# RWKV triangular inverse: the level's mask put on by VectorE on the way out of PSUM, the copies of y by ScalarE

## The chip, the cores and the metric

One core of a Trainium2 chip. The kernel is written by hand: each engine (TensorE or PE, VectorE or DVE, ScalarE or ACT, GpSimd or POOL, SyncE or SP) has its own program, and they meet by semaphores. The metric is the time of one execution in microseconds; lower is better.

## What is computed

Two transformer-like blocks of two layers each over 256 tokens of 1024 features, in float32. The second layer of the first block is an RWKV-7 mixer, and its scan is where the change lies:

```python
def frame_step(state, inp):
    r_t, w_t, k_t, v_t, a_t, b_t = inp
    sa = jnp.einsum('bhvk,bhk->bhv', state, a_t)
    state = (state * w_t[:, :, None, :]
             + sa[..., None] * b_t[:, :, None, :]
             + v_t[..., None] * k_t[:, :, None, :])
    y_t = jnp.einsum('bhvk,bhk->bhv', state, r_t)
    return state, y_t
```

It runs over 256 steps for 16 heads of size 64. All else (convolution mixer, MLPs, attention layers) is the same in both kernels.

## The kernel before

**Chunks and slots.** The scan is done in 4 chunks of 64 steps. Inside a chunk the recurrence is a triangular system, whose 64x64 matrix must be inverted for each head and chunk. The 16 heads go through in 4 slots (`SLOTS`) of 4 heads; a slot's work on 128 partitions has two halves, q = 0 and 1, with 4 chunks each. After the 4 slots a fifth round (slot 4) finishes the last slot's chain.

**The inverse.** The Gram matrix comes from TensorE ("gram" step). VectorE masks it: `xt` becomes the inverse of the 2x2 diagonal blocks (the mask of level 0 and the unit matrix, L1992 and L1994), `nb_t` the strictly triangular matrix N beside the products for y (L1995), and a 32x32-block transpose of `xt` gives `inv_x` (L1996). Then the blocks double, level j = 1 to 5. A level has for each half a step "t1", TensorE: `inv_x` times N, with N cut down to the entries that join two blocks of this level (`n_m`), into PSUM; a copy of it to `t1` in SBUF by ScalarE (L1287); a step "dx", TensorE: `t1` times the late columns of `xt`; an addition to `xt` by VectorE (L2005), and a transpose to `inv_x` for the next level (L2008). TensorE's "t1" of level j + 1 waits for that transpose (`inv_ready`), its "dx" for the copy (`t1_out`). The cut N of level 1 is made by VectorE (L1993), that of levels 2 to 5 by GpSimd from `nb_t` (L817, `nm_ready`).

**The chain.** One slot behind, the chain over the 4 chunks runs between these steps: "rhs", "u", "sy". ScalarE takes the results of "rhs" and "u" out of PSUM (L1293, L1301) and scales the old state (L1298); VectorE makes the new state (L2020, L2022) and copies y out of PSUM, three copies for each chunk (`keep_y`, L1980 and L1982, 48 in all), at the step "u" of the next chunk. "sy" of the next chunk waits for them (`y_out`).

**What sets the order.** `wkv_steps(slot)` is one list of steps which TensorE, ScalarE and VectorE all walk through, each in order and each waiting by semaphore. Other work is hung on places in it. In slot 0 that is, on TensorE, the last value projections (L2252 to L2254), and on VectorE `mixer_inputs(3)`, which prepares slot 3 (L1882 and L1883 after level 1, L1885 and L1887 after level 2, L1889 after level 3, all 128x512), and two halves of weight splits (`w_lo`, L1507, 128x1024, after level 4 and at the end). In slots 1 and 2 there is one such half, between the two "t1" steps of level 3. Slots 2 and 3 have the group norm of finished heads as well (L1965, L1968, L1971, L1974). Slot 4 has the first rows of the output projection, for which VectorE makes `z_lo` (L1956).

**GpSimd** has an order of its own: in each slot the masks of levels 2 to 5, and between them the inputs of the next slot (`build_bk`: L761, L763; `build_ar`: L774 to L776; then it adds to `built`), and after them `gate_products` of this slot (L783, L784, L787), all 128x512 in SBUF.

## Time and profile before

| | us |
|---|---|
| median of 3 runs | 1352.33 |
| lowest, highest run | 1350.98, 1352.74 |
| span of the profiled execution (first to last instruction) | 1350.7 |
| its stretch with slots 0 to 4 of the scan (about 427 to 549 us) | 122 |

The profiled execution lasts 1350.7 us from its first to its last instruction; the median of the runs is 1.6 us more, for what lies around the span. In it slot 0 begins with the gram step at 426.93 us, and slots 1 to 3 begin at 455.02, 478.26 and 503.07 us; the chain of slot 3 begins at 527.7 us. TensorE has the full clock in all of them. A row of the timeline gives the start in microseconds, the duration, the engine and the line; neighbouring instructions of one line are merged into a row with xN; what stands in brackets is the idle time of the engine ahead of the row and what ended it. PE's own rows are modelled and overlap, so that a wait of some tenths of a microsecond can hide in the tail of the row ahead. A few PE records are missing.

### The profile page before, as it was taken

To read this page: it belongs to the slowest core of one execution; us is meant where nothing else is said; L and a number is where in the kernel's file an instruction comes from. 1 tells how busy PE (TensorE), PEld (TensorE's weight loads), DVE (VectorE), ACT (ScalarE), POOL (GpSimd) and SP (SyncE) were. 2 spreads that over 40 slices of the span, in tenths; PEclk is the share of its full clock that TensorE was granted. 3 is DMA by queue.
4 is the path that set the end of the run, shared out by engine and by line. 5 is a ranking of instruction groups with operands and counts; after the bars stand their busy time and mean duration, and the time that the engine had idled before them with its cause. 6 is when DMAs were issued, how large, how long until landed. Compare 5 with 4: busy or idle time off the path is not lost. (4 is left out here: it accounts for less than half of the span.)

```text
span 1350.7 us, 24951 instructions
## 1 busy us (share of the span) xinstructions
PE 1303.9 (97%) x10507; PEld 1130.7 (84%) x10507; DVE 948.4 (70%) x1433; ACT 701.1 (52%) x1211; POOL 128.3 (9%) x133
## 2 busy tenths in 40 slices
PE   4999999999999999999999999999999999999997
PEld 2998888997899887788888887888888998888886
DVE  1887788976768776685556888666657677756655
ACT  2534544434467455564444648654445566644443
POOL 0000000010200864100000142000000021000000
PEclk9999999999999999999999999999999999999999
DMA  9997899995341012356665532465565544565561
GB/s 363 373 366 236 302 350 381 356 344 161 110 156 64 4 35 97 98 178 196 188 192 177 176 121 74 150 203 192 187 196 160 170 143 126 172 188 192 183 197 51
DMA packets 177559, 256.90 MB, mean 190 GB/s; under 512 B 10472, under 2 KB 122536, under 8 KB 177448
## 3 DMA queue, kind: packets, MB, share of 16 engines
q1 hardware_dynamic: 177448, 255.31, 57.0%
q8 instruction: 83, 1.36, 0.4%
q14 instruction: 28, 0.23, 0.0%
HBM read 254.25 MB, written 1.05 MB: 189 GB/s over the span
## 5 line engine op out<-in xcount | busy, mean ns | idle before, releaser
L1507 DVE TENSOR_TENSOR w_lo<-stage,w_hi 128x1024 fp32r<-128x1024 f32 (+1 forms) x372 | 447.3, 1238 | 160.4 <-ACT w_hi L882 160.0
L882 ACT ACTIVATE w_hi<-stage 128x1024 fp32r<-128x1024 f32 (+1 forms) x378 | 379.9, 1049 | 211.7 <-PE acc L2311 191.9
L2309 PE MATMUL acc<-w_hi,z_hi 128*128 128x512 f32 x640 | 252.7, 395 | 1.6 <-DVE z_lo L1956 1.6
L2311 PE MATMUL acc<-w_hi,z_lo 128*128 128x512 f32 x640 | 249.4, 390 | 0.0
L2310 PE MATMUL acc<-w_lo,z_hi 128*128 128x512 f32 x640 | 249.2, 389 | 0.0
L2252 PE MATMUL un<-h_both,w_hi 128*128 128x256 f32 x736 | 214.9, 292 | 1.8 <-POOL w_lo L853 1.1
L2253 PE MATMUL un<-h_both,w_hi 128*128 128x256 f32 x736 | 208.8, 284 | 0.0
L2254 PE MATMUL un<-h_both,w_lo 128*128 128x256 f32 x736 | 208.8, 284 | 0.0
L2252 PEld LDWEIGHTS un<-h_both,w_hi 128*128 128x128 f32 x736 | 141.6, 192 | 9.5 <-issue 5.4
L2309 PEld LDWEIGHTS acc<-w_hi,z_hi 128*128 128x128 f32 x640 | 120.1, 188 | 27.8 <-issue 3.9
L2253 PEld LDWEIGHTS un<-h_both,w_hi 128*128 128x128 f32 x736 | 141.7, 193 | 1.2 <-issue 0.7
L2254 PEld LDWEIGHTS un<-h_both,w_lo 128*128 128x128 f32 x736 | 141.7, 193 | 0.0
L2311 PEld LDWEIGHTS acc<-w_hi,z_lo 128*128 128x128 f32 x640 | 120.1, 188 | 25.4
L2310 PEld LDWEIGHTS acc<-w_lo,z_hi 128*128 128x128 f32 x640 | 120.2, 188 | 23.4
L2290 PE MATMUL un<-h_both,w_hi 128*128 128x512 f32 x384 | 121.2, 397 | 0.4 <-DVE w_lo L1507 0.4
L2290 PE MATMUL side<-h_both,w_hi 128*128 128x512 f32 x384 | 120.8, 396 | 0.4
L2293 PEld LDWEIGHTS side<-h_both,w_lo 128*128 128x128 f32 x384 | 72.1, 188 | 17.0
L2293 PEld LDWEIGHTS un<-h_both,w_lo 128*128 128x128 f32 x384 | 72.1, 188 | 16.9
L2293 PE MATMUL un<-h_both,w_lo 128*128 128x256 f32 x384 | 75.5, 278 | 0.0
L2293 PE MATMUL side<-h_both,w_lo 128*128 128x256 f32 x384 | 75.5, 278 | 0.0
L1789 DVE SCALAR_TENSOR_TENSOR ada_sum<-ada_buf,small,ada_sum 128x1024 f32<-128x1024 f32 x49 | 62.8, 1282 | 1.0
L2290 PEld LDWEIGHTS un<-h_both,w_hi 128*128 128x128 f32 x384 | 59.1, 189 | 1.7 <-DVE w_lo L1507 0.6
(393 smaller groups left out, 1885.1 us busy)
## 6 DMA issues: line engine op xcount, KB each, us to landing
stage<-in_mlp_w SPq DMA_DIRECT2D x64, 1024.0 KB
ada_buf<-in_ada_w SPq DMA_DIRECT2D x48, 1024.0 KB, 11.1
stage<-in_w_up SPq DMA_DIRECT2D x32, 1024.0 KB
stage<-in_w_down SPq DMA_DIRECT2D x32, 1024.0 KB
...
```

Of the source, the lines that this page charges most:

```text
L882: A_(w_hi[u % 2][:, half, 0:n], stage[u % NSTAGE][:, half, 0:n], ACT.Copy).then_inc(hi_made, 1)
L1507: V.tensor_tensor(w_lo[u % 2][:, half, 0:n], stage[u % NSTAGE][:, half, 0:n], w_hi[u % 2][:, half, 0:n].bitcast(F32), ALU.subtract).then_i ...
L1789: V.scalar_tensor_tensor(out=to[:], in0=rows, scalar=by, in1=to[:], op0=ALU.mult, op1=ALU.add).then_inc(ada_weighed, 1)
L2252: MM(out, hi_l, hi_r, start=start, stop=False, skip_group_check=True)
L2253: MM(out, hi_l, lo_r, start=False, stop=False, skip_group_check=True)
L2254: return MM(out, lo_l, hi_r, start=False, stop=stop, skip_group_check=True)
L2290: MM(pair[:, m, :, :], wh[:, kt, c], h_both[:, kt, :, :], start=(kt == 0), stop=False, skip_group_check=True)
L2293: ins = MM(pair[:, m, 0, :], wl[:, kt, c], h_hi[:, kt, :], start=False, stop=(kt == KT - 1), skip_group_check=True)
L2309: MM(y, z_hi[:, kt, q], wh[:, i, :], start=(first and kt == 0), stop=False, skip_group_check=True)
L2310: MM(y, z_hi[:, kt, q], wl[:, i, :], start=False, stop=False, skip_group_check=True)
L2311: ins = MM(y, z_lo[:, kt, q], wh[:, i, :], start=False, stop=(last and kt == KT - 1), skip_group_check=True)
```

## The change

Three things move. The matrix N is no longer cut for each level: TensorE's "t1" takes `nb_t` itself, and the mask of the level (`level_of`, turned) is multiplied onto the product when it leaves PSUM. This multiplication is VectorE's; ScalarE's 40 copies of `t1` go, and so do GpSimd's 32 masks, VectorE's 8 and the buffers `n_m`. The 48 copies of y go from VectorE to ScalarE, at the same steps. GpSimd's other work now stands at the head of its slot. TensorE's instructions stay as they are but for one operand and one wait.

```diff
-    levels = [(s >> (j + 1) == q >> (j + 1)) & ((q >> j) & 1 == 1) & ((s >> j) & 1 == 0) for j in range(6)]
-    put("level_t", np.stack(levels, 1))
+    paired = lambda early, late, j: (early >> (j + 1) == late >> (j + 1)) & ((late >> j) & 1 == 1) & ((early >> j) & 1 == 0)
+    put("level_first", paired(s, q, 0))
+    put("level_of", np.stack([paired(q, s, j) for j in range(1, 6)], 1))
...
@@ -780,10 +780,13 @@
+                pool.wait_ge(built, s + 1)
+                pool.wait_ge(chain_input, 3)
                 link(G.tensor_tensor(rw_c[:, t, :], rw_r[:, t, :], rw_k[:, t, :], ALU.mult))
                 G.tensor_tensor(rw_c[:, t, :], rw_c[:, t, :], spread(VEC_RK), ALU.mult).then_inc(rk_ready, 1)
                 if s == 0:
                     pool.wait_ge(lora2_out, 20)
+                    pool.wait_ge(built, 1)
...
@@ -808,24 +811,15 @@
             for s in range(SLOTS):
-                for j in WKV_LEVELS[1:]:
-                    for q in range(2):
-                        if j == 2:
-                            pool.wait_ge(inv_ready, 12 * s + q + 1)
-                        else:
-                            pool.wait_ge(t1_done, 10 * s + 2 * (j - 3) + q + 1)
-                        G.tensor_tensor(n_m[(j - 1) % 2][:, q, :, :], nb_t[s % 2][:, q, :, 0:CHUNK],
-                                        level_t[:, j, :].unsqueeze(1).to_broadcast([P, CHUNKS, CHUNK]), ALU.mult).then_inc(nm_ready, 1)
-                    if j == (2 if s else 4) and s + 1 < SLOTS:
-                        build_bk(s + 1)
-                    if j == (3 if s else 5) and s + 1 < SLOTS:
-                        build_ar(s + 1)
-                    if j == 4 and s >= 2:
-                        group_weigh(s - 2)
+                if s + 1 < SLOTS:
+                    build_bk(s + 1)
+                    build_ar(s + 1)
+                if s >= 2:
+                    group_weigh(s - 2)
+                gate_products(s)
                 if s >= 2:
                     group_gate(s - 2)
                     group_add(s - 2)
-                gate_products(s)
...
@@ -1273,6 +1267,15 @@
+            def keep_y(s, c):
+
+                act.wait_ge(y_done, CHUNKS * s + c + 1)
+                cols = slice(CHUNK * c, CHUNK * (c + 1))
+                A_(y_wkv[:, 2 * s, cols], two_pairs(misc, P)[:, 0, :], ACT.Copy)
+                for rows, to in zip(HEAD, HEAD[::-1]):
+                    ins = A_(y_wkv[to, 2 * s + 1, cols], two_pairs(misc, P)[rows, 1, :], ACT.Copy)
+                ins.then_inc(y_out, 1)
...
@@ -1283,8 +1286,6 @@
                     elif step == "t1":
-                        act.wait_ge(t1_done, 10 * s + 2 * (j - 1) + q + 1)
-                        A_(t1[:, q, :, :], half_bank(acc[q], 0), ACT.Copy).then_inc(t1_out, 1)
...
@@ -1299,6 +1300,10 @@
                         A_(wkv_u[:], two_pairs(stat_ps, P), ACT.Copy).then_inc(u_out, 1)
+                        if j:
+                            keep_y(s, j - 1)
+                    elif step == "sy" and j == CHUNKS - 1:
+                        keep_y(s, j)
...
@@ -1989,15 +1985,18 @@
-                        V.tensor_tensor(xt, raw_n[:, :, 0:CHUNK], bc4(level_t[:, 0, :], CHUNKS), ALU.mult)
-                        link(V.tensor_tensor(n_m[0][:, q, :, :], raw_n[:, :, 0:CHUNK], bc4(level_t[:, 1, :], CHUNKS), ALU.mult))
-                        V.tensor_tensor(xt, xt, bc4(eye, CHUNKS), ALU.add)
+                        V.tensor_tensor(xt, raw_n[:, :, 0:CHUNK], bc4(level_first, CHUNKS), ALU.mult)
                         link(V.tensor_tensor(nb_t[s % 2][:, q, :, :], raw_n, bc4(c_("masks"), CHUNKS), ALU.mult))
+                        link(V.tensor_tensor(xt, xt, bc4(eye, CHUNKS), ALU.add))
...
+                    elif step == "t1":
+
+                        dve.wait_ge(t1_done, 10 * s + 2 * (j - 1) + q + 1)
+                        V.tensor_tensor(t1[:, q, :, :], half_bank(acc[q], 0), bc4(level_of[:, j - 1, :], CHUNKS), ALU.mult).then_inc(t1_out, 1)
...
@@ -2022,10 +2021,6 @@
-                        else:
-                            keep_y(s, c)
-                    elif step == "u" and j:
-                        keep_y(s, j - 1)
...
@@ -2689,10 +2684,8 @@
                         pe.wait_ge(inv_ready, 12 * s + 2 * (j - 1) + q + 1)
-                        if j > 1:
-                            pe.wait_ge(nm_ready, 8 * s + 2 * (j - 2) + q + 1)
                         for c in range(CHUNKS):
-                            ins = by_head(half_bank(acc[q], 0)[:, c, :], n_m[(j - 1) % 2][:, q, c, :], xn[:, c, :])
+                            ins = by_head(half_bank(acc[q], 0)[:, c, :], nb_t[i][:, q, c, 0:CHUNK], xn[:, c, :])
```

The order on VectorE in slot 0, from the end of `mixer_inputs(2)` to the next piece, before. `acc0` to `acc3` are PSUM banks (0 and 1 hold "t1", 2 and 3 "dx"), `tmp` and `rw0` to `rw5` the mixer's tiles in SBUF:

```order
L1889 SCALAR_TENSOR_TENSOR rw4_115<-rw4_115,rw5_116 128x512
L2005 TENSOR_TENSOR inv_t2_189<-acc2,inv_t2_189 128x64x2 [waits dx_done,chain_input]
L2008 STREAM_TRANSPOSE inv_x_142<-inv_t2_189 128x256 [waits dve_chain]
L2005 TENSOR_TENSOR inv_t2_189<-acc3,inv_t2_189 128x64x2 [waits dx_done]
L2008 STREAM_TRANSPOSE inv_x_142<-inv_t2_189 128x256 [waits dve_chain]
L1882 TENSOR_TENSOR tmp_61<-tmp_61,ss_inv_126 128x512 [waits ss_root,ss_ready]
L1883 SCALAR_TENSOR_TENSOR tmp_61<-tmp_61 128x512 [waits dve_chain]
L2005 TENSOR_TENSOR inv_t2_189<-acc2,inv_t2_189 128x32x4 [waits dx_done,dve_chain]
L2008 STREAM_TRANSPOSE inv_x_142<-inv_t2_189 128x256 [waits dve_chain]
```

and in the changed kernel:

```order
L1894 SCALAR_TENSOR_TENSOR rw4_115<-rw4_115,rw5_116 128x512
L1999 TENSOR_TENSOR t1_150<-acc0,const1_64 128x256 [waits t1_done,chain_input]
L1999 TENSOR_TENSOR t1_150<-acc1,const1_64 128x256 [waits t1_done]
L2004 TENSOR_TENSOR inv_t2_187<-acc2,inv_t2_187 128x64x2 [waits dx_done]
L2007 STREAM_TRANSPOSE inv_x_142<-inv_t2_187 128x256 [waits dve_chain]
L2004 TENSOR_TENSOR inv_t2_187<-acc3,inv_t2_187 128x64x2 [waits dx_done]
L2007 STREAM_TRANSPOSE inv_x_142<-inv_t2_187 128x256 [waits dve_chain]
L1887 TENSOR_TENSOR tmp_61<-tmp_61,ss_inv_126 128x512 [waits ss_root,ss_ready]
L1888 SCALAR_TENSOR_TENSOR tmp_61<-tmp_61 128x512 [waits dve_chain]
L1999 TENSOR_TENSOR t1_150<-acc0,const1_64 128x256 [waits t1_done,dve_chain]
L1999 TENSOR_TENSOR t1_150<-acc1,const1_64 128x256 [waits t1_done]
L2004 TENSOR_TENSOR inv_t2_187<-acc2,inv_t2_187 128x32x4 [waits dx_done]
```

The two multiplications L1999 stand ahead of each level's additions, and behind `mixer_inputs` (L1887 and L1888 here are L1882 and L1883 before).

The order on GpSimd in slot 0, before:

```order
L817 TENSOR_TENSOR n_m1_145<-nb_t0_133,const1_64 128x256 [waits const_mid_in,inv_ready,un_free,rw_ready]
L817 TENSOR_TENSOR n_m1_145<-nb_t0_133,const1_64 128x256 [waits inv_ready]
L817 TENSOR_TENSOR n_m0_144<-nb_t0_133,const1_64 128x256 [waits t1_done] x2
L817 TENSOR_TENSOR n_m1_145<-nb_t0_133,const1_64 128x256 [waits t1_done] x2
L761 TENSOR_TENSOR b_fm_138<-rw4_115,w_inv_141 128x512 [waits tok_done,exp_ready,rw_ready]
L763 TENSOR_TENSOR k_fm_139<-rw1_112,w_inv_141 128x512
L817 TENSOR_TENSOR n_m0_144<-nb_t0_133,const1_64 128x256 [waits t1_done] x2
L774 COPY ar1_143<-rw5_116 128x8
```

and in the changed kernel, where the inputs of slot 1 and then the gate products come first:

```order
L761 TENSOR_TENSOR b_fm_138<-rw4_115,w_inv_141 128x512 [waits rw_ready,exp_ready,const_mid_in,tok_done,un_free]
L763 TENSOR_TENSOR k_fm_139<-rw1_112,w_inv_141 128x512
L774 COPY ar1_143<-rw5_116 128x8
L775 TENSOR_TENSOR ar1_143<-rw5_116,w_cum_140 128x8x63
L776 TENSOR_TENSOR ar1_143<-rw0_111,w_cum_140 128x8x64
L777 ISA [waits pool_chain]
L785 TENSOR_TENSOR rw3_114<-rw0_111,rw1_112 128x512 [waits chain_input,built]
L786 TENSOR_TENSOR rw3_114<-rw3_114,vecT_66 128x512 [waits pool_chain]
L790 TENSOR_TENSOR rw1_112<-sq_62,vecT_66 128x512 [waits built,lora2_out]
```

The eight masks that this piece had between and ahead of them are gone, and nothing in it waits for a level of the inverse.

ScalarE in slot 1, level 3, from the chain's "rhs" of chunk 2 to that of chunk 3, before:

```order
L1293 ACTIVATE wkv_rhs_149<-side 128x128 [waits rhs_done]
L882 ACTIVATE w_hi1_54<-stage1_50 128x1024 [waits unit_done,unit_landed1]
L1287 ACTIVATE t1_152<-acc0 128x256 [waits t1_done]
L1298 ACTIVATE state_kept_148<-state1_147,w_end_151 128x64 [waits state_ready]
L1298 ACTIVATE state_kept_148<-state1_147,w_end_151 128x64
L1301 ACTIVATE wkv_u_150<-side 128x128 [waits u_done]
L1287 ACTIVATE t1_152<-acc1 128x256 [waits t1_done]
L1287 ACTIVATE t1_152<-acc0 128x256 [waits t1_done]
L1293 ACTIVATE wkv_rhs_149<-side 128x128 [waits rhs_done]
```

and in the changed kernel:

```order
L1294 ACTIVATE wkv_rhs_147<-side 128x128 [waits rhs_done]
L876 ACTIVATE w_hi1_54<-stage1_50 128x1024 [waits unit_done,unit_landed1]
L1299 ACTIVATE state_kept_146<-state1_145,w_end_149 128x64 [waits state_ready]
L1299 ACTIVATE state_kept_146<-state1_145,w_end_149 128x64
L1302 ACTIVATE wkv_u_148<-side 128x128 [waits u_done]
L1274 ACTIVATE tmp_61<-side 128x64 [waits y_done]
L1276 ACTIVATE tmp_61<-side 64x64 x2
L1294 ACTIVATE wkv_rhs_147<-side 128x128 [waits rhs_done]
```

Three copies of y now stand behind `wkv_u`, and the copies of `t1` are gone.

## Rows read from the trace of the kernel before

**Rows 1.** The page, busy time of the engines, with the number of their instructions.

```profile
PE 1303.9 (97%) x10507; PEld 1130.7 (84%) x10507; DVE 948.4 (70%) x1433; ACT 701.1 (52%) x1211; POOL 128.3 (9%) x133
```

**Rows 2.** Windows, slots 0 to 3: length; PE, PEld, DVE, ACT, POOL busy; clock; DMA.

```profile
426.93:455.02 28.09, 27.37 (x574) 25.29 (x574) 23.42 (x43) 17.56 (x36) 14.09 (x14) 1.00 0.01 3
455.02:478.26 23.24, 21.05 (x712) 19.96 (x709) 18.32 (x51) 12.21 (x33) 18.38 (x19) 1.00 0.03 5
478.26:503.07 24.81, 22.76 (x722) 21.31 (x719) 18.67 (x52) 14.43 (x38) 14.18 (x15) 1.00 0.12 46
503.07:527.14 24.07, 22.73 (x720) 21.22 (x716) 18.91 (x53) 12.75 (x35) 12.92 (x14) 1.00 0.05 7
```

**Rows 3.** Groups by line and shape, 426 to 545 us: busy, mean ns | idle before.

```profile
L817 POOL TENSOR_TENSOR n_m<-nb_t,const 128x256 f32<-128x256 f32 x32 | 25.7, 820 | 102.6 <-DVE inv_x L1996 89.5 <-PE acc L2642 12.9
...
L1287 ACT ACTIVATE t<-acc 128x256 f32<-128x256 f32 x40 | 15.3, 383 | 30.3 <-PE acc L2642 30.0
...
L1982 DVE COPY tmp<-side 64x64 f32<-64x64 f32 x30 | 6.7, 222 | 0.4
...
L1301 ACT ACTIVATE wkv_u<-side 128x128 f32<-128x128 f32 x15 | 4.1, 275 | 5.7 <-PE side L2642 5.6
...
L1993 DVE TENSOR_TENSOR n_m<-acc,const 128x256 f32<-128x256 f32 x8 | 3.3, 409 | 0.0
...
L1980 DVE COPY tmp<-side 128x64 f32<-128x64 f32 x15 | 3.1, 208 | 2.2 <-PE side L2642 2.1
```

**Rows 4.** Timeline of slot 0, ScalarE: start, microseconds, line, operation.

```profile
437.83 0.62 ACT L1141 ACTIVATE w_inv<-rw 128x512 f32<-128x512 f32 x1
...
440.17 0.38 ACT L1287 ACTIVATE t<-acc 128x256 f32<-128x256 f32 x1 [1.72 <-PE acc L2642]
```

**Rows 5.** Timeline of slot 0, VectorE.

```profile
438.89 0.68 DVE L1889 SCALAR_TENSOR_TENSOR rw<-rw,rw 128x512 f32<-128x512 f32 x1
...
442.85 0.65 DVE L1882 TENSOR_TENSOR tmp<-tmp,ss_inv 128x512 f32<-128x512 f32 x1
...
443.53 0.69 DVE L1883 SCALAR_TENSOR_TENSOR tmp<-tmp 128x512 f32<-128x512 f32 x1
...
444.89 0.29 DVE L2005 TENSOR_TENSOR inv_t<-acc,inv_t 128x128 f32<-128x128 f32 x1 [0.67 <-PE acc L2642]
...
446.24 1.04 DVE L1885 SCALAR_TENSOR_TENSOR rw<-rw,tmp 128x512 f32<-128x512 f32 x1
...
447.32 1.64 DVE L1887 SCALAR_TENSOR_TENSOR rw<-ka_mix,rw 128x512 f32<-128x512 f32 x1
...
450.22 0.70 DVE L1889 SCALAR_TENSOR_TENSOR rw<-rw,rw 128x512 f32<-128x512 f32 x1
```

**Rows 6.** Timeline of slot 0, GpSimd and TensorE.

```profile
446.69 1.72 POOL L763 TENSOR_TENSOR k_fm<-rw,w_inv 128x512 f32<-128x512 f32 x1
...
444.12 1.12 PE L2642 MATMUL acc<-inv_t,t 64*64 64x32 f32 x32
```

**Rows 7.** Timeline of slot 1, VectorE and, last, TensorE.

```profile
457.61 0.41 DVE L1992 TENSOR_TENSOR inv_t<-acc,const 128x256 f32<-128x256 f32 x1
...
462.05 0.43 DVE L2020 TENSOR_SCALAR state<-side,w_end 128x64 f32<-128x64 f32 x2
...
462.40 1.28 DVE L2000 TENSOR_TENSOR nk_t<-acc,const 128x512 f32<-128x512 f32 x2
...
463.40 0.61 PE L2642 MATMUL acc<-inv_t,t 64*64 64x32 f32 x16
```

**Rows 8.** Timeline of slots 1 to 4, VectorE.

```profile
470.01 1.25 DVE L1507 TENSOR_TENSOR w_lo<-stage,w_hi 128x1024 fp32r<-128x1024 f32 x1 [0.33 <-ACT w_hi L882]
...
497.85 0.68 DVE L1968 SCALAR_TENSOR_TENSOR rw<-un,rw 128x512 f32<-128x512 f32 x1
...
505.04 1.13 DVE L1994 TENSOR_TENSOR inv_t<-inv_t,const 128x256 f32<-128x256 f32 x1
...
530.84 3.20 DVE L1956 TENSOR_TENSOR z_lo<-rw,z_hi 128x512 fp32r<-128x512 f32 x2
```

More of the change, by code:

```diff
@@ L49 @@
 CONST_PARTS = ((("ident", P), ("mean", P), ("ones", P), ("rot", P)),
-               (("head_ones", P), ("head_mean", P), ("level_t", 6 * CHUNK), ("masks", 2 * CHUNK), ("eye", CHUNK), ("resets", SEQ),
+               (("head_ones", P), ("head_mean", P), ("level_first", CHUNK), ("level_of", 5 * CHUNK), ("masks", 2 * CHUNK), ("eye", CHUNK), ("resets", SEQ),
                 ("eye_centered", CHUNK)),
@@ L169, in build @@
         ident, mean_w, ones_w, head_ones, head_mean, rot_w = (c_(n) for n in ("ident", "mean", "ones", "head_ones", "head_mean", "rot"))
-        level_t = c_("level_t").rearrange("p (j q) -> p j q", j=6)
+        level_first, level_of = c_("level_first"), c_("level_of").rearrange("p (j q) -> p j q", j=5)
         eye, eye_centered = c_("eye"), c_("eye_centered")
@@ L259, in build @@
         ar.append(scratch_new("ar1", DOUBLE))
-        n_m = [scratch_new(f"n_m{i}", PACKED) for i in range(2)]
         state = [scratch_new(f"state{i}", [P, 2, HD]) for i in range(2)]
@@ L712, in build @@
             sem(n) for n in ("g_done", "v_done", "gk_done", "tok_done", "tok_out", "inv_ready", "lak_ready", "chain_input"))
-        nm_ready, t1_done, t1_out, dx_done = (sem(n) for n in ("nm_ready", "t1_done", "t1_out", "dx_done"))
+        t1_done, t1_out, dx_done = (sem(n) for n in ("t1_done", "t1_out", "dx_done"))
         rhs_done, rhs_out, u_done, u_out, y_done, y_out, s_done, state_ready = (
@@ L1974, in group_step @@
                     V.scalar_tensor_tensor(out=rw_k[:, t, :], in0=rw_k[:, t, :], scalar=-0.5, in1=s, op0=ALU.mult, op1=ALU.mult).then_inc(scaled, 1)
-            def keep_y(s, c):
-                dve.wait_ge(y_done, CHUNKS * s + c + 1)
-                cols = slice(CHUNK * c, CHUNK * (c + 1))
-                V.tensor_copy(y_wkv[:, 2 * s, cols], two_pairs(misc, P)[:, 0, :])
-                for rows, to in zip(HEAD, HEAD[::-1]):
-                    ins = V.tensor_copy(y_wkv[to, 2 * s + 1, cols], two_pairs(misc, P)[rows, 1, :])
-                ins.then_inc(y_out, 1)
             for slot in range(SLOTS + 1):
```

## The prediction

> **What bounds the kernel now.** I read the page first, then the windows of the scan's slots, then the timeline slot by slot. On the page TensorE is busy for 97% of the span [rows 1], so time is won or lost only where TensorE waits, or is kept waiting longer. The change touches nothing outside the scan. In its slots TensorE's rows cover 27.4 of 28.1, 21.1 of 23.2, 22.8 of 24.8 and 22.7 of 24.1 us [rows 2], about 6 us open in all, and VectorE's 23.4, 18.3, 18.7 and 18.9 us: it is the second engine, well ahead of ScalarE (17.6, 12.2, 14.4, 12.8 us). The reader is to see that the change takes work from engines with room (GpSimd 14 to 18 us a slot, ScalarE) and puts 40 instructions on the one with least room, inside the loop that releases TensorE. After the scan TensorE's work goes on without a gap that could take up a delay; I let a shift go through to the end.
>
> **The prices.** A multiplication of the mask is a VectorE tensor_tensor with one operand in PSUM, 128x256. L1993 is exactly that: 0.41 us [rows 3]. ScalarE's copy takes 0.38 [rows 3], so the exchange by itself costs TensorE 0.03 us. VectorE gets 40 x 0.41 = 16.4 us, and loses 8 x 0.41 = 3.3 and 16 copies of y at 0.21 + 2 x 0.22 = 0.65, 10.4 us: net +2.7 us. But slot 0 has no copies of y, and gets 10 x 0.41 - 2 x 0.41 = +3.3 us on 23.4 of 28.1. ScalarE loses 15.3 us, and gets the copies of y; the trace has no ScalarE copy of 64 columns. Its nearest row is `wkv_u`, 128 columns, 0.28 us [rows 3]: at most 3 x 0.28 = 0.83 a chunk, at least VectorE's 0.65; I take 0.7. [...] GpSimd loses 25.7 us of masks [rows 3]. The waits name no GpSimd instruction that TensorE waited for, so this gives nothing directly; what it does to VectorE comes below.
>
> **Slot 0, VectorE in the loop.** Before, ScalarE copied `t1` at 440.17 [rows 4], and while VectorE was in `mixer_inputs` ScalarE did level 2's copies beside it: "dx" could go at 444.12 [rows 6], though VectorE was in L1882 and L1883 from 442.85 to 444.22 [rows 5]. Now these multiplications stand behind them in VectorE's queue. A level becomes a serial piece: first multiplication 0.41, then "dx" to the first addition 444.12 to 444.89 = 0.77 [rows 5, 6], then two additions and two transposes, 444.89 to 446.24 = 1.35 [rows 5]: 2.53 us, the second multiplication and the second "dx" lying inside. From the first product at 440.15: four levels, 10.1; the last without transposes, 0.41 + 0.77 and 0.65 for two additions, 1.85; the mixer pieces 1.37, 1.37 and 0.69; two weight splits at 1.25 [rows 8]. Sum 17.9, so gram of slot 1 would begin on VectorE at 458.05 and not at 457.61 [rows 7]: +0.45.
>
> That is without GpSimd. L1887 took 1.64 us where its like take 0.69; GpSimd's L763 ran until 446.69 + 1.72 = 448.41, and L1887 ended 0.55 behind that [rows 5, 6]. L763 itself had waited for L1885. So such a pair, both reading two operands from SBUF, goes by turns. The change starts GpSimd's stream for slot 1 when `w_inv` is there, 438.45 [rows 4], where L763, the second piece of it, started at 446.69 before. It has no more masks to break it: seven pieces of 1.05 to 1.2 us (L763's 1.72 less its wait) and a short copy, until about 449. By turns I get: L1889, due 438.89 [rows 5], ends at 440.7 (the first multiplication 0.55 late); level 1 to 443.25; L1882 by 443.95, L1883 waits for L776 until 445.2 and ends at 445.75; level 2 to 448.3; L1885 waits for the last gate product until 449.1, L1887 ends at 450.3; level 3 452.8; L1889 453.5; level 4 456.05; split 457.3; level 5 459.15; split 460.4. Against 457.61 that is +2.8. The ends from the rows: VectorE loses nothing where it comes first (L1889 at 450.22, 0.70 us [rows 5]), +0.45; it loses L1887's 0.95 at each of the five meetings, +0.45 + 4.75 = +5.2. I take the walk, since its turns are those of L1885 and L1887.
>
> [...]
>
> **Slots 1 to 3.** The gram step loses L1993 twice, 0.8 us. But "dx" of level 1 must now wait behind the new state, both `nk_t` and a multiplication. Before: gram begins 457.61, its last transpose makes way at 462.05, `nk_t` begins 462.40 for 1.28, "dx" goes at 463.40, 5.8 after the start [rows 7]. Now: 4.44 - 0.8 + 0.35 + 1.25 + 0.4 = 5.65. The 0.8 us are nearly all given back: -0.15. The weight split between the two "t1" steps of level 3 (470.01, 1.25 us [rows 8]) now stands ahead of a multiplication too. Before, the same copy stood on ScalarE behind its own share of that split, so it was late too; I take 0.3 of the 1.25 as new. The copies of y on ScalarE stay hidden, as two steps lie between "u" and "sy". Slot 1 is +0.15 in all, and slot 2 +0.2, where the group's work leaves TensorE less to wait for. L1968 (0.68 us [rows 8]) stands behind the second multiplication of level 4 in slots 2 and 3, which waits for its product; the addition behind it comes some 0.4 late: +0.3 and +0.4. Slot 3 begins with GpSimd on the group's sum, its weights and the gate products, five pieces or some 6 us in a row; L1994 met one of them before (1.13 for 0.43 [rows 8]), and now both halves do, 0.6 + 0.7 for 0.7: +0.6; the copies of y that VectorE drops at the end of the slot give back 0.4. Slots 1 to 3: 0.15 + 0.5 + 0.6 = +1.25.
>
> **Slot 4.** `z_lo` took 3.20 us for two because GpSimd's gate products ran [rows 8]; these are done earlier now, so 1.4. TensorE had other work for most of it: -0.35.
>
> **Sum.** +2.8 + 1.25 - 0.35 = +3.7 us on a span of 1350.7; the median of the runs is 1.6 above the span, so 1352.3 + 3.7 = 1356.0 us. Its own range is 1354.6 to 1358.
>
> **The rivals.**
> *The locks miss.* If GpSimd's pieces fall between VectorE's, slot 0 costs 0.45 and slot 3 nothing: 0.45 + 0.8 - 0.35 = +0.9, 1353.2 us. For it: L1889 at 450.22 was not stretched [rows 5], though GpSimd ran. Against: GpSimd has no gap for 10 us and VectorE comes to it five times.
> *The cleared gram step is kept (faster).* If "dx" of level 1 in slots 1 to 3 is not held by VectorE but by the transpose alone, the 0.8 us stay in each: -2.4; with slot 4's -0.35, L1994's 0.7 of slot 3 [rows 8] gone as well, and slot 0 even: -3.45, 1348.9 us. It decides at whether VectorE comes to the multiplication before TensorE has its level 1 product and "rhs" behind it, that is within 1.3 us of the last transpose (462.05 to 463.40); I count 0.35 + 1.25 + 0.4 = 2.0 [rows 7].
> *ScalarE holds the chain (slower still).* `y_out` comes 0.7 us after `u_out` now, and "sy" needs it at its start and not at its middle. If that is exposed at half of the 12 places in slots 1 to 4 that have a chain step behind, 6 x 0.5 = +3 on top: 1359 us. Against: two steps of TensorE lie between.
>
> **The numbers.** Main case 0.52, locks miss 0.24, faster 0.12, slower still 0.12. About 0.2%, 2.7 us, is what a measurement of this kernel can tell from no change. The main case lies above 1355.0 for the most part (0.45 of 0.52), so slower is 0.45 + 0.12 + 0.02 = 0.59; same 0.07 + 0.22 = 0.29; faster 0.12. The range 1351.8 to 1358.8 leaves out the faster case and half of the last.
>
> **What would show it.** Slot 1's gram step on TensorE begins near 458.5 in the span's time (455.02 before), if slot 0 is right; VectorE's L1883 (now L1888) of slot 0 lasts about 1.8 us and shows the lock, 0.7 would show that it misses. In slot 1 the distance from gram's first VectorE row to the first "dx" is 5.65 us; 5.0 would be the faster rival. `z_lo` in slot 4 takes 1.4 us. Waits of TensorE for `tmp` of ScalarE at "sy" would show the last rival. I am wrong at the root if TensorE's waits in slot 0 stay under 1 us, or if a multiplication takes much else than 0.41 us.

## The result and the profile after

The changed kernel is slower: 1358.07 us median of four runs (1357.15 to 1362.24) beside 1352.26 for the kernel before on the same chip, a ratio of 1.0052, 95% interval 1.0036 to 1.0067, so +5.8 us where +3.7 was forecast. The direction was right, the size too small; the time lies inside the range by 0.7 us, and only since the range reached toward the slowest rival.

The profiled execution of after is the slowest of the four (span 1360.5 us, against 1350.7 before; its mean granted clock is 0.993, that of the other three 0.995 or 0.996), so it shows more loss than the median has. The table compares the stage slot by slot, from VectorE's first gram row of a slot to that of the next; the last column runs from slot 3's first gram row to the row of VectorE that begins the chain's last new state in slot 4.

| us | slot 0 | slot 1 | slot 2 | slot 3 and chain |
|---|---|---|---|---|
| before | 29.42 | 21.91 | 24.73 | 37.55 |
| after | 34.87 | 22.21 | 25.39 | 38.36 |
| difference | +5.45 | +0.30 | +0.66 | +0.81 |

That is +7.2 us, three quarters of it in slot 0. Another 1.0 us lies ahead of the stage and some 1.6 behind it, where both kernels run the same instructions; behind the stage the profiles of all kernels here spread by 3 us, so the 1.6 says nothing on the change.

The windows of after: slot 0, slot 1, and four pieces of slot 0 (length; busy PE, PEld, DVE, ACT, POOL; granted clock; DMA).

```profile
428.00:462.50 34.50, 31.20 (x578) 29.27 (x582) 27.29 (x51) 15.11 (x26) 9.08 (x8) 0.85 0.01 3
462.50:485.10 22.60, 20.58 (x714) 19.74 (x712) 18.43 (x47) 10.36 (x33) 8.39 (x8) 1.00 0.02 4
...
444.00:448.00 4.00, 1.29 (x42) 1.15 (x38) 3.86 (x4) 0.00 (x0) 3.77 (x3) 0.98 0.00 0
448.00:452.00 4.00, 4.00 (x54) 3.71 (x54) 2.74 (x6) 0.00 (x0) 1.03 (x2) 0.50 0.01 2
452.00:456.00 4.00, 4.00 (x56) 3.81 (x52) 2.90 (x7) 0.00 (x0) 0.00 (x0) 0.50 0.02 4
456.00:458.00 2.00, 2.00 (x37) 1.91 (x38) 0.42 (x1) 0.00 (x0) 0.00 (x0) 0.50 0.00 0
```

Before, slot 0 had TensorE busy for 27.37 of 28.09 us at clock 1.00 [rows 2]. Now two things are there that were not. From 444 to 448 TensorE is busy for 1.29 of 4 us. Behind it the granted clock is 0.50 for 10 us (0.85 over 34.5 us says the same: 34.5 x 0.15 / 0.5 = 10.4).

What TensorE waited for stands in the timeline of after, GpSimd, VectorE and TensorE around 444 us:

```profile
443.65 1.27 POOL L776 TENSOR_TENSOR ar<-rw,w_cum 128x512 f32<-128x512 f32 x1
445.07 1.52 POOL L785 TENSOR_TENSOR rw<-rw,rw 128x512 f32<-128x512 f32 x1 [0.15 <-POOLq L777]
...
443.88 1.59 DVE L1887 TENSOR_TENSOR tmp<-tmp,ss_inv 128x512 f32<-128x512 f32 x1
445.50 1.63 DVE L1888 SCALAR_TENSOR_TENSOR tmp<-tmp 128x512 f32<-128x512 f32 x1
447.17 0.76 DVE L1999 TENSOR_TENSOR t<-acc,const 128x256 f32<-128x256 f32 x2
...
443.79 1.15 PE L2637 MATMUL acc<-inv_x,nb_t 64*64 64x64 f32 x32
447.65 1.05 PE L2637 MATMUL acc<-inv_t,t 64*64 64x32 f32 x18 [2.71 <-DVE t L1999]
```

L1887 and L1888, the mixer's pieces, took 0.65 and 0.69 us before [rows 5]. Each now ends 0.55 us behind the end of the GpSimd instruction that runs at its start (444.92 and 446.59). The multiplication L1999 stands behind them in VectorE's queue, and "dx" starts 3.86 us after "t1" did, with 2.71 us of idle time.

In slot 1 the gram step is 0.8 us lighter, and the first "dx" comes no earlier than before: 469.91 - 464.08 = 5.83 us (5.79 before [rows 7]). VectorE's first gram row, its `nk_t` and its multiplication, and TensorE's "dx":

```profile
464.08 0.42 DVE L1988 TENSOR_TENSOR inv_t<-acc,const 128x256 f32<-128x256 f32 x1
...
468.15 1.28 DVE L1995 TENSOR_TENSOR nk_t<-acc,const 128x512 f32<-128x512 f32 x2
469.35 0.75 DVE L1999 TENSOR_TENSOR t<-acc,const 128x256 f32<-128x256 f32 x2
...
469.91 0.50 PE L2637 MATMUL acc<-inv_t,t 64*64 64x32 f32 x11 [0.59 <-DVE t L1999]
```

The copies of y on ScalarE (`tmp` is where y is kept), and "sy" that waits for them, later in slot 1:

```profile
475.40 1.05 ACT L876 ACTIVATE w_hi<-stage 128x1024 fp32r<-128x1024 f32 x1
476.35 0.57 ACT L1299 ACTIVATE state_kept<-state,w_end 128x64 f32<-128x64 f32 x2
476.83 0.26 ACT L1302 ACTIVATE wkv_u<-side 128x128 f32<-128x128 f32 x1
476.99 0.22 ACT L1274 ACTIVATE tmp<-side 128x64 f32<-128x64 f32 x1
477.21 0.45 ACT L1276 ACTIVATE tmp<-side 64x64 f32<-64x64 f32 x2
...
477.72 0.45 PE L2637 MATMUL side<-v_tok,bk_tok 64*64 64x64 f32 x8 [0.65 <-ACT tmp L1276]
```

The groups of after by line, in the stage (busy, mean ns | idle before):

```profile
L1999 DVE TENSOR_TENSOR t<-acc,const 128x256 f32<-128x256 f32 x40 | 16.3, 417 | 9.1 <-PE acc L2637 8.8
L1276 ACT ACTIVATE tmp<-side 64x64 f32<-64x64 f32 x32 | 7.0, 219 | 0.4
...
L2637 PEld LDWEIGHTS side<-v_tok,bk_tok 64*64 64x64 f32 x96 | 3.8, 134 | 2.8 <-ACT tmp L1276 2.7
L1274 ACT ACTIVATE tmp<-side 128x64 f32<-128x64 f32 x16 | 3.5, 219 | 2.7 <-PE side L2637 2.7
```

Before, the same weight loads of "sy" stood idle for 0.8 us, of which 0.4 for VectorE's copies of y:

```profile
L2642 PEld LDWEIGHTS side<-v_tok,bk_tok 64*64 64x64 f32 x96 | 3.9, 134 | 0.8 <-DVE tmp L1982 0.4 <-issue 0.3
```

### The profile page after: what moved, and what is told of

It reads as the page before. It is cut to its first block and busy times, and to the rows that moved or that the text cites. A ratio compares the mean times of both kernels' runs of the same rounds, so it can differ in the third digit from the quotient of the medians.

```text
span 1360.5 us, 24884 instructions
## 1 busy us (share of the span) xinstructions
PE 1308.1 (96%) x10507; PEld 1135.0 (83%) x10507; DVE 949.8 (70%) x1417; ACT 697.9 (51%) x1219; POOL 102.9 (8%) x101
## 3 DMA queue, kind: packets, MB, share of 16 engines
HBM read 254.25 MB, written 1.05 MB: 188 GB/s over the span
```

## Experiments

Theory A: slot 0 is long because GpSimd's stream stretches VectorE's pieces, the multiplication comes late, TensorE waits, and the clock falls behind that wait. Rivals: VectorE's queue alone does it (B); the clock has another cause (C). More rivals, with letters of their own, stand with the run that tests them. For slots 1 to 4: ScalarE's copies of y hold the chain (E), or VectorE's sum of work is the price (F). The totals are medians, with the kernel before run beside them on the same chip; the slots are read from one profiled execution of each kernel.

| kernel | us, before beside it | ratio, 95% | slot 0 | slot 1 | slot 2 | slot 3 and chain |
|---|---|---|---|---|---|---|
| pool_late | 1355.00, 1351.48 | 1.0025 (1.0016 to 1.0034) | 30.04 | 22.21 | 25.37 | 38.37 |
| warm | 1364.17, 1351.48 | 1.0086 (1.0072 to 1.0100) | 35.85 | 22.21 | 27.40 | 38.37 |
| warm3 | 1358.51, 1351.99 | 1.0047 (1.0034 to 1.0059) | 31.57 | 22.21 | 25.61 | 38.39 |
| b_idle | 1356.47, 1350.95 | 1.0038 (1.0026 to 1.0050) | 32.49 | 21.85 | 24.62 | 37.54 |
| moved | 1355.56, 1351.99 | 1.0026 (1.0015 to 1.0037) | 29.97 | 22.25 | 25.50 | 38.35 |
| moved_late | 1354.13, 1351.99 | 1.0019 (1.0010 to 1.0027) | 28.72 | 22.25 | 25.77 | 38.36 |
| moved_split | 1354.33, 1351.99 | 1.0019 (1.0010 to 1.0027) | 28.71 | 22.94 | 24.93 | 38.35 |
| y_back | 1359.09, 1351.48 | 1.0059 (1.0047 to 1.0072) | 33.53 | 22.87 | 25.94 | 39.04 |
| b_y_act | 1354.40, 1351.48 | 1.0024 (1.0015 to 1.0033) | 29.43 | 22.63 | 25.41 | 38.33 |
| y_first | 1356.19, 1351.31 | 1.0037 (1.0023 to 1.0051) | 32.37 | 22.04 | 25.12 | 37.83 |
| b_y_first | 1353.30, 1351.31 | 1.0012 (1.0003 to 1.0021) | 29.43 | 23.58 | 24.82 | 37.78 |
| b_all | 1352.37, 1351.31 | 1.0010 (1.0001 to 1.0018) | 29.20 | 23.59 | 25.28 | 37.79 |
| inter | 1357.93, 1351.87 | 1.0048 (1.0034 to 1.0062) | 32.34 | 21.62 | 25.38 | 37.76 |
| all_three | 1352.38, 1351.31 | 1.0008 (0.9999 to 1.0016) | 28.72 | 22.07 | 24.86 | 37.80 |
| four | 1352.04, 1351.87 | 1.0005 (0.9996 to 1.0013) | 29.19 | 21.79 | 24.74 | 37.23 |
| four_s | 1351.81, 1350.95 | 1.0004 (0.9996 to 1.0013) | 28.70 | 21.80 | 25.00 | 37.21 |
| five | 1351.00, 1350.95 | 0.9997 (0.9988 to 1.0006) | 28.38 | 22.49 | 24.87 | 37.24 |

### GpSimd's stream late (pool_late)

```diff
             for s in range(SLOTS):
+                if s == 0:
+                    pool.wait_ge(t1_done, 6)
                 if s + 1 < SLOTS:
                     build_bk(s + 1)
                     build_ar(s + 1)
```

> The changed kernel with one edit: in slot 0 GpSimd starts its stream (inputs of slot 1, then gate products) only when the two products of level 3 are there, as late as the masks of the kernel before let it. Theory A (the lock and what it does to the clock): L1887 and L1888 of slot 0 last 0.69 us each and not 1.59 and 1.63, TensorE's wait ahead of the second level's "dx" falls from 2.7 us to about 1, and its granted clock stays at 1.00 through slot 0; the later pieces of GpSimd meet L1894 and the weight split and cost about 1 us. Slot 0 lasts 29 to 30 us and not 34.5, the total is 1353 to 1354.5 us. Rival B (VectorE's queue is enough): the pieces standing ahead of the multiplications starve TensorE with or without GpSimd, the clock falls all the same, slot 0 stays over 33 us and the total at 1357 or more.

Slot 0 is 30.04 us long, at the upper end of what Theory A gave, and the total 0.5 us above its range. The clock is 1.00 throughout. VectorE's pieces at level 2 and GpSimd's first one, in its timeline (the line numbers are two higher here):

```profile
442.90 0.65 DVE L1889 TENSOR_TENSOR tmp<-tmp,ss_inv 128x512 f32<-128x512 f32 x1
443.59 0.69 DVE L1890 SCALAR_TENSOR_TENSOR tmp<-tmp 128x512 f32<-128x512 f32 x1
...
448.21 1.26 POOL L761 TENSOR_TENSOR b_fm<-rw,w_inv 128x512 f32<-128x512 f32 x1 [95.32 <-PE acc L2639]
```

With no GpSimd beside them the same two instructions take 1.34 and not 3.22 us. Rival B falls: 4.8 us of the profiled slot 0 come and go with the order of GpSimd alone.

### The wait filled, and the clock with it (warm, warm3)

```diff
+                if n == 9:
+                    pe.wait_ge(tok_out, 4)
+                    unread(un[0], 3)
                 if n in (7, 11, 15, 19):
                     value_rows(3, misc, ...)
```

(`warm` has 8 for 3; `n == 9` is the second "t1" of level 2.)

> The changed kernel with eight matmuls of 128x512 more on TensorE between level 2's "t1" and "dx" of slot 0, into a free PSUM bank that nothing reads: they fill the wait and alter no data. VectorE and GpSimd do the same work as in the changed kernel. Theory A (the wait itself costs what the walk said, and the clock the rest): the clock stays at 1.00 in slot 0, L1887 and L1888 still take 1.6 us each, slot 0 lasts 28.1 + 2.8 = 31 us, the total is 1354 to 1355 us. Rival C (the fall of the clock has nothing to do with this wait, or the later waits bring it as well): half clock is still seen in slot 0 and the total stays at 1357 to 1358.5. Rival D (the matmuls hold the chain up): at half a microsecond each they could last longer than the wait, then "dx" starts later than 447.8 and the total is above 1358.

Rival D came true: sixteen rows of 0.45 us lasted 7.13 us, "dx" started only at 453.04, and slot 0 took 35.85 us, at clock 1.00. (Its slot 2 is long, 27.40 us, for a fall of its own: the clock is 0.61 from 492 to 496 us.) So three were taken:

> As the run with eight added matmuls, but three of them in the same place: eight lasted 7.13 us (sixteen rows of 0.45) and outlasted the wait, three make 2.7 us, which is TensorE's wait there in the changed kernel (444.94 to 447.65). VectorE and GpSimd do what they do in the changed kernel, and "dx" starts when it did. Theory A (the waits cost what the walk said, the fall of the clock costs the rest): the granted clock stays 1.00 in slot 0, slot 0 (from VectorE's first gram row to that of slot 1) lasts 31.5 us and not 34.87, and the total is 3.3 us under that of the changed kernel, some 1354 us. Rival C (this wait doesn't decide the clock): half clock is still seen before slot 1, slot 0 stays over 34 us, the total within 1 us of the changed kernel's.

The timeline of warm3, VectorE and TensorE, and its windows (as above):

```profile
444.87 1.59 DVE L1887 TENSOR_TENSOR tmp<-tmp,ss_inv 128x512 f32<-128x512 f32 x1
446.50 1.64 DVE L1888 SCALAR_TENSOR_TENSOR tmp<-tmp 128x512 f32<-128x512 f32 x1
...
445.87 2.84 PE L2351 MATMUL un<-const 128*128 128x512 f32 x6
448.65 1.06 PE L2640 MATMUL acc<-inv_t,t 64*64 64x32 f32 x30
...
429.00:460.20 31.20, 29.69 (x584) 26.16 (x588) 26.82 (x51) 15.11 (x26) 9.08 (x8) 1.00 0.01 3
...
450.00:454.00 4.00, 3.29 (x74) 2.98 (x73) 3.47 (x10) 0.00 (x0) 0.04 (x1) 1.00 0.02 6
```

VectorE and GpSimd do exactly what they do in after, "dx" comes 3.78 us behind L1887's start (3.77 in after), only TensorE is not idle meanwhile. The clock stays at 1.00, and slot 0 takes 31.57 us, not 34.87. This splits slot 0's +5.45 in the profiled executions: the waits cost 31.57 - 29.42 = 2.15 us, the half clock 3.3 us. Rival C falls.

The total did not come down as Theory A had it: 1358.5 us, where 1354 was expected. So the 3.3 us rest on one profile of each kernel, and no median shows them. The profiled execution begins the stage 2.0 us late, with a clock of 0.67 between 340 and 344 us, long before anything that differs. The profiles of warm, y_back and five show a fall at the same place (0.66, 0.59 and 0.69), those of the other kernels, before and after among them, do not, so it does not come from the added matmuls. The fastest run (1356.17 us, mean clock 0.998) is what the slot lengths give (1352 + 4.2). The others had 0.996 or 0.997. Why the clock falls there in some executions and not in others is open.

### The same wait in the kernel before (b_idle)

```diff
                     elif step == "t1":
                         act.wait_ge(t1_done, 10 * s + 2 * (j - 1) + q + 1)
+                        for _ in range(6 if (s, j, q) == (0, 2, 0) else 0):
+                            link(A_(t1[:, q, :, :], half_bank(acc[q], 0), ACT.Copy))
                         A_(t1[:, q, :, :], half_bank(acc[q], 0), ACT.Copy).then_inc(t1_out, 1)
```

> The kernel before with ScalarE's first copy of t1 at level 2 of slot 0 done seven times over instead of once (same data each time), some 3 us more between that "t1" and its "dx". Masks, GpSimd's order and VectorE's pieces are those of the kernel before, so nothing is stretched but this one wait of TensorE. Theory A (a wait of this size in slot 0 brings the granted clock down to half behind it): TensorE waits 2.5 to 3.5 us there, half clock of 3 to 10 us follows, slot 0 is longer by the wait and 1 to 3 us more; total +4 to +6. Rival C (the clock needs the changed kernel's other waits too): clock 1.00, slot 0 longer by 2.5 to 3 us and no more.

Its timeline, ScalarE's six copies and TensorE's "dx", and two windows:

```profile
443.83 2.46 ACT L1288 ACTIVATE t<-acc 128x256 f32<-128x256 f32 x6 [1.87 <-PE acc L2644]
...
446.76 1.12 PE L2644 MATMUL acc<-inv_t,t 64*64 64x32 f32 x32 [2.51 <-ACT t L1289]
...
444.00:448.00 4.00, 1.49 (x43) 1.31 (x38) 0.81 (x3) 2.79 (x8) 4.00 (x4) 0.97 0.00 0
448.00:452.00 4.00, 3.95 (x60) 3.62 (x62) 2.36 (x6) 0.97 (x3) 1.39 (x3) 0.60 0.02 4
```

A wait of 2.51 us, with nothing else changed, and the clock is at half behind it. Theory A holds for the cause. The median rose by 5.5 us, about twice the wait. Slot 0 grew by 3.07 us, the wait and 0.6 more, under the 1 to 3 that Theory A gave: this execution had half clock for 3.2 us only. All six runs took 1353.8 to 1358.8 us, and their mean clocks order them: 0.997 for the two fastest, 0.995 for the next three, 0.994 for the slowest.

### Pieces out of slot 0 (moved, moved_late, moved_split)

```diff
-                if slot == 0 and n in (7, 11, 15):
-                    mixer_inputs(3, (n // 4 - 1,))
+                if slot == 0 and n in (7, 11):
+                    mixer_piece(3, (0, 3)[(7, 11).index(n)])
+                if slot == 1 and n in (13, 25, 31):
+                    mixer_piece(3, (1, 2, 4)[(13, 25, 31).index(n)])
```

(`mixer_piece(k, i)` is instruction i of the five of `mixer_inputs`. The first and fourth read `ss_inv` and `ka_mix`, whose memory slot 1 writes over.)

> The changed kernel with mixer_inputs(3) taken apart: in slot 0 only L1887 (after level 1) and L1892 (after level 2) stay, L1888, L1890 and L1894 go to slot 1, after level 1's second addition, between level 4's "t1" steps and between level 5's, where VectorE waits for 0.4 to 0.7 us. GpSimd's order stays as in the changed kernel. Theory A: VectorE has one piece less to meet GpSimd with at level 2, L1887 still takes 1.6 us but L1888 is gone, TensorE's wait there is 1.1 us and not 2.7, the clock stays at 1.00: slot 0 about 29.5 to 30.5, slot 1 some 0.5 us longer, total 1353.5 to 1354.5. Rival B (one stretched piece is enough): the clock falls all the same, over 1356.

> Both edits together: the pieces in slot 1 as in that run, and GpSimd's stream of slot 0 held until level 3's products. Theory A: no piece is stretched at level 2, slot 0 has 2.05 us less of VectorE's work on its loop than with the late stream alone (30.04 us there) and lasts 28.5 to 29, slot 1 0.5 longer than 22.2; total 0.5 to 1.5 us under that with the late stream alone, 1353.5 to 1354.5. Rival G (slot 1 has no room: each piece there delays a multiplication for its whole 0.69 us): what slot 0 gives, slot 1 takes, total as with the late stream alone.

> As moved_late, and slot 1's half of a weight split (1.23 us, between level 3's "t1" steps) put between level 5's "t1" steps, and the three pieces in slot 1 after level 1's and level 2's additions and between level 4's "t1" steps. If VectorE's waits are what hides such pieces, level 3's second multiplication comes 1.2 us earlier and level 5's 0.5 later: slot 1 0.4 to 0.7 us shorter than in moved_late. If TensorE has other steps to do there anyway, no difference.

In moved L1887 is still stretched (1.60 us), but L1888 is gone from behind it, and TensorE waits 1.05 us instead of 2.71; the clock is 1.00, slot 0 takes 29.97 us. One stretched piece was not enough for the fall, against Rival B of this run; the total, 1355.56 us, is all the same 1.1 us above what Theory A gave. In moved_late slot 0 is 28.72 us, shorter than before, and slot 1 takes the three pieces for nothing (22.25 for 22.21), though slot 2 has 0.4 us more. Against pool_late that is -1.3 us in slot 0 and -1.4 in the total, each total taken against the kernel before beside it. moved_split gives the same total. Slot 1 was to be 0.4 to 0.7 us shorter by the split's new place and is 0.69 longer; slot 2 gains 0.84, so nothing follows on that split.

### Who copies y, and when (y_back, b_y_act, y_first, b_y_first)

> The changed kernel with the copies of y given back to VectorE, at their old places; the rest as changed. Theory E (ScalarE's copies hold the chain): the waits of TensorE for ScalarE ahead of "sy" (0.65, 0.64, 0.93, 1.13 us in the changed kernel) go, slots 1 to 4 are 1 to 2 us shorter, 1356 to 1357 us. Theory F (VectorE is the engine to spare, as the prediction had it): VectorE gets 10.4 us more in slots 1 to 4, each copy group of 0.65 us stands ahead of a multiplication, and about half is exposed, +3 to +5, 1361 to 1363 us. Slot 0 has no copies of y and stays at 34.5 us.

> The kernel before with only the copies of y moved to ScalarE; masks, GpSimd's order and ScalarE's copies of t1 as before. ScalarE then has both kinds of copies. Theory E (ScalarE's place in the chain costs): a copy group of 0.67 us stands behind the copy for "u" and ahead of a copy of t1, so +1 to +3 us in slots 1 to 4, 1353.5 to 1355 us. Theory F (relief of VectorE counts): -1 to -2, 1350.5 to 1351.5 us. Slot 0 stays at 28.1 us with the clock at 1.00 by both.

y_back is the changed kernel with `keep_y` on VectorE again, b_y_act the kernel before with it on ScalarE, as in the diff of the change. With y back on VectorE, slots 1 to 4 take 0.66 + 0.55 + 0.68 = 1.9 us more than after: the copies' move is right once the multiplications are on VectorE, though F's +3 to +5 was too much. In the kernel before the same move costs 0.72 + 0.68 + 0.78 = 2.2 us: there ScalarE has the copies of `t1` as well. So neither E nor F alone; each holds where its engine is the one in the loop. And the rest of the change (the multiplications, with the masks gone and GpSimd's new order) costs, in slots 1 to 4, y_back against before: 0.96 + 1.21 + 1.49 = 3.7 us.

```diff
-                        act.wait_ge(u_done, CHUNKS * s + j + 1)
-                        A_(wkv_u[:], two_pairs(stat_ps, P), ACT.Copy).then_inc(u_out, 1)
                         if j:
                             keep_y(s, j - 1)
+                        act.wait_ge(u_done, CHUNKS * s + j + 1)
+                        A_(wkv_u[:], two_pairs(stat_ps, P), ACT.Copy).then_inc(u_out, 1)
```

> The changed kernel with one edit on ScalarE: the copies of y of the chunk before go ahead of the copy for "u", not behind it. Their product is ready right behind that of "rhs" (TensorE's last_of_y), and ScalarE waits there for TensorE's "u" (0.98, 1.12 us in slot 1 of the changed kernel). Theory E (it was the place of the copies on ScalarE that held "sy", 0.65 us at a time): "sy" waits no longer for the copies of y, each of the slots 1 to 3 and the chain after them is 0.3 to 0.8 us shorter, 1 to 2 us in all; slot 0 as in the changed kernel with its half clock. Rival H (the copy for "u" now comes 0.67 us late and "sy" waits for that): no change or slower.

> The kernel before with the copies of y on ScalarE, ahead of the copy for "u"; all else as before. With the copies behind it (b_y_act) slots 1 to 4 took 2.4 us more than before. Theory E: most of it goes, total within 1 us of the kernel before, perhaps below it, as VectorE has 10 us less to do. Rival I (the 0.67 us in front of ScalarE's copies of t1 are the price, wherever they stand): it stays at +2 to +3 us.

With the copies ahead, the weight loads of "sy" wait 1.2 us for ScalarE's copies and not 2.7; the group in y_first:

```profile
L2637 PEld LDWEIGHTS side<-v_tok,bk_tok 64*64 64x64 f32 x96 | 3.8, 134 | 1.9 <-ACT tmp L1276 1.2 <-issue 0.7
```

Slots 1 to 4 are 0.17 + 0.27 + 0.53 = 1.0 us shorter than after. That is the lower end of the 1 to 2 expected, and Rival H falls. The ratio is 1.0037 for 1.0052, but the profiled slot 0 had less half clock too (32.37 us), so the totals do not measure this edit. b_y_first stands 2.0 us over the kernel before beside it, b_y_act 2.9: E for a part, I for the rest. b_y_first's profiled slot 1 is 0.95 us longer than b_y_act's, with a clock of 0.57 from 462 to 466 us. TensorE's wait ahead of it and the windows around it, first of b_y_first, then of b_y_act:

```profile
461.83 0.68 PE L2642 MATMUL acc<-inv_x,n_m 64*64 64x64 f32 x16 [1.50 <-DVE inv_x L2000]
...
460.00:462.00 2.00, 0.50 (x16) 0.36 (x14) 1.93 (x6) 0.87 (x2) 0.55 (x2) 1.00 0.00 0
462.00:466.00 4.00, 4.00 (x89) 4.00 (x88) 2.19 (x6) 2.38 (x9) 4.00 (x5) 0.57 0.02 4
```

```profile
461.89 0.68 PE L2642 MATMUL acc<-inv_x,n_m 64*64 64x64 f32 x16 [1.50 <-DVE inv_x L2000]
...
460.00:462.00 2.00, 0.50 (x17) 0.36 (x15) 1.93 (x6) 0.87 (x2) 0.55 (x2) 1.00 0.00 0
462.00:466.00 4.00, 4.00 (x126) 3.79 (x128) 2.86 (x8) 2.72 (x10) 4.00 (x5) 1.00 0.02 4
```

The same wait of 1.50 us, with TensorE as little busy around it, was followed by the fall in one and not in the other. The profiles of before and b_idle have this wait too and keep 1.00; b_all's has it and falls to 0.64. So a shorter wait than slot 0's can bring the clock down, in some executions and not in others; what decides is open.

b_all moved pieces on top of b_y_first:

> As b_y_first, and three pieces of mixer_inputs(3) moved to slot 1 as in moved. VectorE's loop in slot 0 of the kernel before has TensorE busy for 27.4 of 28.1 us, so at most 0.7 us can be won there; GpSimd's L763 no longer meets L1887 there (1.64 for 0.69 us), but masks and pieces meet in slot 1. Theory: slot 0 0.3 to 0.7 us shorter, slot 1 even; total 0.5 us under b_y_first. Rival: the pieces hold slot 1's loop for as much as slot 0 gains, no difference.

Slot 0 gained 0.23 us, the ratio 1.0010 for 1.0012: no difference that could be told.

### The first "dx" of a slot (inter)

```diff
                     elif step == "tok":
+                        if q == 0:
                             dve.wait_ge(gk_done, s + 1)
                             V.tensor_tensor(nk_t[s % 2][:, q, :, :], ..., ALU.mult).then_inc(lak_ready, 1)
                     elif step == "t1":
                         V.tensor_tensor(t1[:, q, :, :], ..., ALU.mult).then_inc(t1_out, 1)
+                        if j == 1 and q == 0:
+                            V.tensor_tensor(nk_t[s % 2][:, 1, :, :], ..., ALU.mult).then_inc(lak_ready, 1)
```

> The changed kernel with one swap on VectorE: in each slot the mask of the second half of nk_t goes behind the first multiplication of level 1 and not ahead of it. In the changed kernel TensorE waits 0.59 us ahead of the first "dx" for that multiplication in slots 1 and 3, 5.83 us after VectorE's first gram row. Theory J (the prediction's slot 1: VectorE's gram step plus nk_t plus multiplication sets the first "dx"): the first "dx" comes 0.6 us earlier, 5.2 us after the first gram row, slots 1 to 3 are 0.3 to 0.6 us shorter each, 1 to 1.8 us in all. Rival K (TensorE's second "dx" then waits for nk_t's second half, or the levels behind are bound by VectorE's sum of work, not by its start): slot lengths stay within 0.2 us. Slot 0 keeps its wait and its half clock by both, so the total may vary with that by 2 us.

VectorE's first gram row and its new order, and TensorE's first "dx" in slot 1:

```profile
460.69 0.41 DVE L1988 TENSOR_TENSOR inv_t<-acc,const 128x256 f32<-128x256 f32 x1
...
464.77 0.68 DVE L1996 TENSOR_TENSOR nk_t<-acc,const 128x512 f32<-128x512 f32 x1
465.37 0.41 DVE L2000 TENSOR_TENSOR t<-acc,const 128x256 f32<-128x256 f32 x1
465.70 0.68 DVE L2002 TENSOR_TENSOR nk_t<-acc,const 128x512 f32<-128x512 f32 x1
...
465.93 0.48 PE L2640 MATMUL acc<-inv_t,t 64*64 64x32 f32 x10
```

5.24 us and not 5.83, and the slot is 0.59 us shorter; slot 3 with the chain gains 0.60, slot 2 nothing (TensorE has 1.4 us there on which only "issue" is named, in both kernels). Theory J holds in two slots of three, 1.2 us in all where 1 to 1.8 was expected. Slot 0 keeps its wait (2.25 us here) and its half clock, and the total stayed with that of after.

### Adding up (all_three, four, four_s, five)

> The changed kernel with the three edits together: GpSimd's stream of slot 0 late, three of the five pieces of mixer_inputs(3) in slot 1, the copies of y ahead of the copy for "u". If the three causes add up: slot 0 28.7 us, slots 1 to 4 1 to 2 us shorter than in moved_late, total 1352 to 1353 us, within 0.1% of the kernel before. If the copies' place is no cause, 1354, as moved_late.

> All four edits: GpSimd's late stream and three pieces moved to slot 1, copies of y ahead of the copy for "u", and the swap of nk_t's second half with the first multiplication. all_three measured 1352.4 us beside 1351.3 of the kernel before. Theory J: 1 to 1.8 us less than all_three, 1350.5 to 1351.5 us, at or just below the kernel before. Rival K: as all_three, 1352.4.

> As four, with the swap of nk_t's second half and the first multiplication in slots 1 to 3 alone. In slot 0 the swap has nothing to win (TensorE has value rows there); slot 0 was 29.19 us in four and 28.72 without the swap. Expected: slot 0 back at 28.7, the rest as in four, total 0.4 us less, 1351.3 to 1351.7 beside 1351.9 of the kernel before. If the 0.47 is scatter of the run, no difference.

> As four_s, with the half of a weight split that stands at slot 0's end (1.34 us on VectorE ahead of slot 1's first gram row) moved into slot 1, behind level 2's first multiplication. Expected by the loop's view: slot 0 0.8 to 1.0 us shorter, slot 1 0.4 to 0.8 longer, total -0.2 to -0.4 against four_s. Rival: VectorE's slot 1 is full by now (three pieces and two halves of splits) and gives back more than slot 0 gained, total above four_s.

all_three has the late stream, the moved pieces and the early copies of y; four adds the swap, four_s makes the swap in slots 1 to 3 only, five also moves the split from slot 0's end into slot 1 (VectorE finished it at 457.5 us in all_three, with slot 1's gram step right behind it), and the first of the three moved pieces from level 1 to level 2. all_three comes to 1.0008, as expected. From there each step is smaller than its interval: 1.0005, 1.0004, 0.9997. four was to be 1 to 1.8 us under all_three and at most 1351.5 us; its slots 1 to 4 are 1.0 us shorter, its slot 0 is 0.5 longer, and it took 1352.04. four_s has slot 0 back at 28.70 us, as expected, and the 0.4 us don't show in the total; in five slot 0 gained 0.3 us more, where 0.8 to 1.0 was expected, and slot 1 gave 0.7 back. five is level with the kernel before, 1351.00 beside 1350.95 us; its slot 0 is 1.0 us shorter than before, its slot 1 0.6 longer. No version was below both kernels by more than can be measured. So the causes found account for the loss within what can be told, and with all of them taken away the change is worth nothing against the kernel before. What can be told is coarse: the slots of four_s are together 0.9 us shorter than before, its total is 0.9 us longer, and from the end of the last new state to the end of the span the profiles of all kernels take 806.8 to 810.0 us for the same instructions.

## Why the prediction was too small

**Slot 0, the waits: right.** The walk gave +2.8, with VectorE's L1888 at about 1.8 us; it took 1.63, and the waits at full clock cost 2.15 (warm3). What the prediction and the expectation of pool_late call "the lock" is, as far as the traces show it, this: L1887 and L1888 took 1.59 and 1.63 us beside GpSimd (after), 0.65 and 0.69 us without it (pool_late), and ended 0.55 and 0.54 us behind the end of the GpSimd instruction that ran at their start. That every such pair goes by turns, as the walk had it, was the author's estimate from L1885 and L1887 in the trace of before; no run shows it as a rule.

**Slot 0, the clock: the step that failed.** The term of the sum that was mis-sized is "against 457.61 that is +2.8". It took waits as time and nothing more. What a wait does to the clock was put at nothing, without a reason; the rows it went by had the full clock in all slots [rows 2]. But the walk itself put the first multiplication of level 2 behind L1882 and a stretched L1883, at 445.75, while TensorE's "t1" was long done; in the run both pieces were stretched, and the wait was 2.71 us, where the longest in the stage of before is 1.5. The term measured +5.45 in the profiled run: 2.15 of waits, 3.3 of half clock. Behind the same wait the profiles of y_first and y_back have less of it (slot 0 32.37 and 33.53 us, so 0.8 and 2.0 over warm3's 31.57). For the median an estimate is 5.8 - 2.15 - 1.8 (slots 1 to 4, below) = 1.9 us. In after's slot 0 a product of 32 matmuls ("t1") took 1.97 us at 450.96 and at 456.10, with the clock at 0.50, and 1.15 us at 443.79, with the clock at 1.00. "The locks miss" was wrong, and its "for it" (one unstretched L1889) was weak evidence.

**The gram step: right.** 5.65 us to the first "dx" was forecast, 5.83 measured, 5.0 would have been the faster rival. inter shows the mechanism by taking 0.59 us of it away.

**Prices: right.** A multiplication took 0.417 us (0.41 forecast), a chunk's copies of y on ScalarE 3 x 0.219 = 0.66 (0.7).

**Slots 1 to 4: too low.** +1.25 - 0.35 = +0.9 was forecast, +1.8 measured. "The copies of y on ScalarE stay hidden, as two steps lie between" failed: by y_first at least 1.0 us of them was exposed. The rival "ScalarE holds the chain" had the mechanism and the waits (TensorE's weight loads wait for `tmp` at "sy" six times, 2.7 us in all, where it had 6 x 0.5) but not their price: y_first took 1.5 us of these waits away, and the slots became 1.0 us shorter. Where GpSimd meets slot 3's gram step L1990 took 0.72 and 1.11 us for 0.42, so 1.0 us against 0.7 of before; the forecast had +0.6 for it. (The forecast's slot 3 also leaves out the -0.15 that it gives to a gram step in slot 1; nothing hangs on that.) Slot 4's `z_lo` went as forecast (1.28 us for two, 1.4 said), but gave nothing to the end that could be seen.

**The cases** were made from waits alone. A second effect of the same wait, of the same size as the wait, was in none of them; that the slowest rival stood near 1359 is no credit to it, since its mechanism gave 1.0 us where it was tested, and not 3.
